# Scan levels on array quarters with idle products, squares summed on VectorE, and expert rows skipped

## The reference

```
h = rms_norm(x) * (1 + scale1) + shift1;  p = h @ w_in
# y_a: RWKV-7 time mixing, 8 heads of 64, both directions
state = state * w_t + (state @ -kk_t) (kk_t * a_t)^T + v_t k_t^T;  y_t = state @ r_t
# y_b: latent attention, 8 heads
q = rms_norm(c_q) @ w_uq;  k, v = rms_norm(c_kv) @ w_uk, w_uv;  y_b = softmax(q k^T) v @ w_o
x = x + gate1 * ((g_a * y_a + g_b * y_b) @ w_out)
# mixture of experts: 4 groups of 8, one group and then 2 experts per token
h2 = rms_norm(x) * (1 + scale2) + shift2
y_e = (silu(h2 @ w13[e][gate]) * (h2 @ w13[e][up])) @ w2[e];  x = x + gate2 * sum of 2 weighted y_e
```

## Time and profile before

| what | value |
| --- | --- |
| median of 3 runs | 2740.32 us (2726.66 to 2760.95) |
| the profiled execution | 2732.23 us, span 2730.4, mean granted TensorE clock 0.93 |
| modulation_and_norm | 0 to 137 us |
| project_in | 137 to 822 us |
| wkv_scan | 831 to 1376 us |
| mla_project | 1380 to 1566 us |
| attention | 1571 to 1886 us |
| finish_and_merge, output_and_router | 1886 to 2261 us |
| routing | 2261 to 2321 us |
| experts, 34 blocks | 2321 to 2662 us |
| end of experts, combine | 2662 to 2731 us |
| busy, whole span | PE 2433.9 us (89%), PEld 1962.5 (72%), DVE 1595.7 (58%), ACT 1062.4 (39%), POOL 677.5 (25%) |
| DMA | 433.31 MB, 122.73 MB of it written; zero stores 32 x 512 KB, 18.2 us from issue to landing |

### The profile page before, as it was taken

How to read it: one execution, slowest core, us unless ns; L and a number is a source line. 1 busy time by engine, 2 the same in 40 slices (tenths; PEclk the granted TensorE clock), 3 DMA queues, 4 the chain that set the end, 5 groups by cost and what they waited for, 6 DMA issues and landing times. The chain is left out here.

```text
span 2730.4 us, 52710 instructions
## 1 busy us (share of the span) xinstructions
PE 2433.9 (89%) x22191; PEld 1962.5 (72%) x22191; DVE 1595.7 (58%) x2165; ACT 1062.4 (39%) x1865; POOL 677.5 (25%) x498
## 2 busy tenths in 40 slices
PE   5799999999994999999979889998997994999990
PEld 2488887788884999999869756665876883666760
DVE  4444469966652354555445566666886445677756
ACT  5311133344441345445445455554122220555542
POOL 1122245545432345434213320001200000000004
PEclk8899999999995699999869989999998995999995
DMA  8422234443324132332043391103755123999977
GB/s 360 172 77 78 78 106 146 142 158 133 140 110 156 45 88 69 88 92 65 19 133 109 101 326 51 33 24 113 245 164 195 69 70 140 400 422 418 414 298 300
DMA packets 178735, 433.31 MB, mean 159 GB/s; under 512 B 38298, under 2 KB 90298, under 8 KB 160834
## 3 DMA queue, kind: packets, MB, share of 16 engines
q1 hardware_dynamic: 148548, 323.10, 34.1%
q0 software_dynamic: 15840, 57.54, 5.5%
q10 hardware_dynamic: 14112, 49.29, 4.5%
HBM read 307.15 MB, written 122.73 MB: 157 GB/s over the span
## 5 line engine op out<-in xcount | busy, mean ns | idle before, releaser
L99 PE MATMUL ps_in<-h_t_low,w_in_high 128*128 128x512 f32 x960 | 379.6, 395 | 10.5 <-POOL w_in_low L490 10.5
L100 PE MATMUL ps_in<-h_t_high,w_in_low 128*128 128x512 f32 x960 | 374.6, 390 | 0.0
L101 PE MATMUL ps_in<-h_t_high,w_in_high 128*128 128x512 f32 x960 | 374.6, 390 | 0.0
L99 PEld LDWEIGHTS ps_in<-h_t_low,w_in_high 128*128 128x128 f32 x960 | 180.7, 188 | 53.0 <-POOL w_in_low L490 11.5
L1191 POOL TENSOR_TENSOR wkv_levels<-wkv_nt,level_mask 128x1024 f32<-128x1024 f32 x60 | 140.1, 2353 | 274.5 <-ACT wkv_nt L1140 274.5
L101 PEld LDWEIGHTS ps_in<-h_t_high,w_in_high 128*128 128x128 f32 x960 | 180.6, 188 | 38.2
L100 PEld LDWEIGHTS ps_in<-h_t_high,w_in_low 128*128 128x128 f32 x960 | 180.8, 188 | 36.0
L2963 DVE TENSOR_TENSOR w_low<-w_now,w_high 128x2048 fp32r<-128x2048 f32 x64 | 146.7, 2292 | 39.3 <-ACT w_high L2800 39.3
L598 ACT COPY p_row<-ps_in 128x512 f32<-128x512 f32 x72 | 42.3, 588 | 304.5 <-PE ps_in L101 278.9
L2670 POOL DMA_INDIRECT xb<-h,row_ids x34 | 32.9, 967 | 511.1 <-PE ps_xy L2715 285.4
L488 POOL CAST w_in_high<-w_in_tile 128x1024 fp32r<-128x1024 f32 x40 | 46.6, 1164 | 335.8 <-PE ps_in L101 299.5
(11 more groups left out here) (383 smaller groups left out, 5788.9 us busy)
## 6 DMA issues: line engine op xcount, KB each, us to landing
w_now<-in_w SPq DMA_DIRECT2D x68, 1024.0 KB, 9.5
w_tile<-in_w SPq DMA_DIRECT2D x34, 1024.0 KB, 9.4
w_ada_tile<-in_w_ada SPq DMA_DIRECT2D x12, 2048.0 KB, 12.3
wkv_in<-wkv_out SPq DMA_DIRECT2D x24, 1024.0 KB, 3.9
w_in_tile<-in_w_in SPq DMA_DIRECT2D x40, 512.0 KB, 3.6
yb<-yb_tile ACTq DMA_DIRECT2D x34, 512.0 KB, 9.3
yb<-att_zeros POOLq DMA_DIRECT2D x32, 512.0 KB, 18.2
p_t<-p_mixed ACTq DMA_DIRECT2D x24, 512.0 KB, 2.7
```

The lines of the kernel that those rows point to most:

```text
L99: nc.tensor.matmul(out, w[0], x[1], start=start, stop=False)
L100: nc.tensor.matmul(out, w[1], x[0], start=False, stop=False)
L101: return nc.tensor.matmul(out, w[0], x[0], start=False, stop=stop)
```

## The change

In the scan the level products go to 32x32 quarters of the array: 64 matmuls per group instead of 32, and `lev`, `nt`, `z` and the mask become half as wide, for only the two diagonal blocks of a chunk matter at levels 0 to 4. `half_product` takes its block from `lbm`. keep_z becomes one copy, keep_nt four, first_inverse one operation. `keep_busy` issues matmuls whose results nobody reads: `idle` at j < 0 and `dense` (one) behind seven of nine groups at j >= 0. Sums of latent squares are added over the blocks on VectorE, so one matmul per sum remains. The zero stores go; `yb` is now indexed by choice and token (3072 rows), the experts' gather and a new scatter skip rows whose index is out of bounds, and combine loads plain 1 MB tiles. The merge gets 12 idle products ahead of it, routing 10 and 6. Cut to its core:

```
 def wkv_scan
-        lmask = s.sb("level_mask", [P, LEVELS, CH])
+        lmask = s.sb("level_mask", [P, LEVELS, BLK])
-        nt = s.sb("wkv_nt", [P, 2, 2 * H, CH])
-        lev = s.sb("wkv_levels", [P, LEVELS, 2 * H, CH])
+        nt = s.sb("wkv_nt", [P, 2, 2 * H, BLK])
+        lev = s.sb("wkv_levels", [P, LEVELS, 2 * H, BLK])
-        z = s.sb("wkv_z", [P, 2 * H, CH])
+        z = s.sb("wkv_z", [P, 2 * H, BLK])
...
+def keep_busy(nc, consts, out, n):
+
+    for _ in range(n):
+        nc.tensor.matmul(out, consts["ident"][:], consts["p_end"][:].rearrange("p d f n -> p (d f n)"), start=True, stop=True)
...
             def level_z(i, l):
                 for h in range(2 * H):
-                    for c in range(2):
-                        mm = nc.tensor.matmul(LV[half(c), 0, h], lev[half(c), l, h], x[half(c), i % 2, h], start=True, stop=True)
+                    for a in quads:
+                        mm = nc.tensor.matmul(LV[a, 0, h], lev[a, l, h], x[a, i % 2, h], start=True, stop=True)
                 mm.then_inc(m["z_full"], 1)
...
             def level_xz(i, l):
                 for h in range(2 * H):
-                    for c in range(2):
-                        mm = nc.tensor.matmul(LV[half(c), 1, h], z[half(c), h], xt[half(c), i % 2, h], start=True, stop=True)
+                    for a in quads:
+                        mm = nc.tensor.matmul(LV[a, 1, h], z[a, h], xt[a, i % 2, h], start=True, stop=True)
                 mm.then_inc(m["xz_full"], 1)
...
+            def idle(j, n):
+
+                if j < 0:
+                    keep_busy(nc, consts, W[:].rearrange("p h t -> p (h t)")[:, 0:2 * RF * TOK // CH], n)
+
+            def dense(j):
+
+                if j >= 0:
+                    keep_busy(nc, consts, W[:].rearrange("p h t -> p (h t)")[:, 0:2 * RF * TOK // CH], 1)
+
+            idle(-2, 20)
             for j in range(-2, N):
                 seq, inner, ahead = j >= 0, 0 <= j + 1 < N, j + 2 < N
                 if inner:
+                    idle(j, 24)
                     level_z(j + 1, 1)
+                    dense(j)
+                    idle(j, 3)
                 if seq:
                     from_state(j, 0)
                 if inner:
                     level_xz(j + 1, 1)
+                    dense(j)
+                    idle(j, 3)
                 if seq:
                     from_values(j, 0)
...
             def keep_z(i, l):
                 act.wait_ge(m["z_full"], 4 * i + l)
-                nc.scalar.mul(z[:, :, 0:BLK], LV[:, 0], blk[:, 0:1])
-                nc.scalar.mul(z[:, :, BLK:CH], LV[:, 0], blk[:, 1:2]).then_inc(m["z_kept"], 1)
+                nc.scalar.copy(z[:], LV[:, 0]).then_inc(m["z_kept"], 1)
...
             def keep_nt(i):
                 act.wait_ge(m["lbm_ready"], 4 * i + 4)
                 if i >= 2:
-                    act.wait_ge(m["half_full"], i - 1)
                     act.wait_ge(m["lev_ready"], LEVELS * (i - 1))
                 for c in range(2):
-                    ins = nc.scalar.copy(nt[half(c), i % 2].rearrange("p (d h) t -> p d h t", d=2),
-                                         lbm[half(c), i % LB].rearrange("p (d c) h t -> p d c h t", d=2)[:, :, c, :, CH * c:CH * c + CH])
+                    for b in range(2):
+                        at = CH * c + BLK * b
+                        ins = nc.scalar.copy(nt[quad(c, b), i % 2].rearrange("p (d h) t -> p d h t", d=2),
+                                             lbm[quad(c, b), i % LB].rearrange("p (d c) h t -> p d c h t", d=2)[:, :, c, :, at:at + BLK])
                 ins.then_inc(m["nt_ready"], 1)
...
-                nc.gpsimd.tensor_tensor(xt[:, i % 2], ident32[:].unsqueeze(1).to_broadcast([P, 2 * H, BLK]), lev[:, 0, :, 0:BLK], ALU.subtract).then_inc(m["x1_part"], 1)
-                pool.wait_ge(m["x1_part"], i + 1)
-                nc.gpsimd.tensor_tensor(xt[:, i % 2], xt[:, i % 2], lev[:, 0, :, BLK:CH], ALU.subtract).then_inc(m["xt_first"], 1)
+                nc.gpsimd.tensor_tensor(xt[:, i % 2], ident32[:].unsqueeze(1).to_broadcast([P, 2 * H, BLK]), lev[:, 0], ALU.subtract).then_inc(m["xt_first"], 1)
...
 def mla_project
             def latent_sums(t, b):
                 if b == 0:
-                    pe.wait_ge(m["squared"], t + 1)
+                    pe.wait_ge(m["lat_added"], t + 1)
                     if t >= 1:
                         pe.wait_ge(m["lat_var"], t)
-                first, n = ((0, QF), (QF, KVF))[b]
-                for k in range(n):
-                    at = 2 * (t % 2) + b
-                    mm = nc.tensor.matmul(ps_st[:, at:at + 1], lat_sq[:, t % 2, first + k], consts["ones"][:, 0:1], start=(k == 0), stop=(k == n - 1))
+                at = 2 * (t % 2) + b
+                mm = nc.tensor.matmul(ps_st[:, at:at + 1], lat_sum[:, t % 2, b], consts["ones"][:, 0:1], start=True, stop=True)
                 if b == 1:
                     mm.then_inc(m["sums_full"], 1)
...
+            def add_squares(t):
+                dve.wait_ge(m["squared"], t + 1)
+                if t >= 2:
+                    dve.wait_ge(m["sums_full"], t - 1)
+                for b, at in enumerate((slice(0, QF), slice(QF, L))):
+                    ins = nc.vector.tensor_reduce(lat_sum[:, t % 2, b], lat_sq[:, t % 2, at].rearrange("p k t -> p t k"), AX.X, ALU.add)
+                ins.then_inc(m["lat_added"], 1)
...
 def attention
-            nc.gpsimd.memset(zeros[:], 0.0).then_inc(zeroed, 1)
-            pool.wait_ge(zeroed, 1)
-            pool.wait_ge(v_loaded[PAIRS - 1], 16)
-            for n in range(TOK * TOP // MB, BLOCKS):
-                pool.dma_start(dram["yb"][n], zeros[:]).then_inc(zeros_stored, 16)
-            pool.wait_ge(zeros_stored, 16 * (BLOCKS - TOK * TOP // MB))
...
 def finish_and_merge
+            keep_busy(nc, consts, ps_b[:].rearrange("p f t -> p (f t)")[:, 0:2 * RF * TOK // CH], 12)
...
 def route_and_experts
+            nc.gpsimd.memset(xb[:], 0.0).then_inc(m["cleared"], 1)
+            pool.wait_ge(m["cleared"], 1)
             pool.wait_ge(m["ids"], 1)
-
-            def gather(t, b, offset):
-                pool.indirect_dma_start(out=xb[:, b], out_offset=None, in_=dram["h2"],
-                                        in_offset=bass.IndirectOffsetOnAxis(ap=offset.bitcast(U32), axis=0)).then_inc(x_in[b], 16)
-
-            for t in range(STATIC):
-                if t >= 2:
-                    pool.wait_ge(m["turned"], t - 1)
-                gather(t, t % 2, ids[:, t:t + 1])
+            rows_at = lambda offset: bass.IndirectOffsetOnAxis(ap=offset.bitcast(U32), axis=0)
+
+            def gather(b, offset):
+                pool.indirect_dma_start(out=xb[:, b], out_offset=None, in_=dram["h2"], in_offset=rows_at(offset),
+                                        bounds_check=TOK - 1, oob_is_err=False).then_inc(x_in[b], 16)
+
+            def scatter(b, offset):
+                pool.indirect_dma_start(out=dram["yb"], out_offset=rows_at(offset), in_=yb[:, b], in_offset=None,
+                                        bounds_check=TOP * TOK - 1, oob_is_err=False).then_inc(stored[b], 16)
+
+            def store(t):
+                pool.wait_ge(m["y_act"], t + 1)
+                pool.wait_ge(m["y_dve"], t + 1)
+                scatter(t % 2, row_to[:, t:t + 1])
+
+            for t in range(STATIC + 4):
+                if t < STATIC:
+                    if t >= 2:
+                        pool.wait_ge(m["turned"], t - 1)
+                    gather(t % 2, row_from[:, t:t + 1])
+                if t >= 4:
+                    store(t - 4)
...
+            def keep_busy(n):
+
+                for _ in range(n):
+                    nc.tensor.matmul(ps_xy[0][:, 0, 0:NTABLES], consts["ident"][:], consts["tables"][:], start=True, stop=True)
+
+            keep_busy(10)
             for k in range(TOP):
                 pe.wait_ge(m["hot_rows"], k + 1)
                 for c in range(T * k, T * k + T):
                     mm = nc.tensor.matmul(ps_ids[:, 0:BLOCKS], row_hot[:, c], block_hot[:, c], start=(c == 0), stop=(c == KT - 1))
             mm.then_inc(m["ids_full"], 1)
+            keep_busy(6)
...
-                act.wait_ge(m["y_act"], t + 1)
-                act.wait_ge(m["y_dve"], t + 1)
-                act.dma_start(dram["yb"][bass.ds(at, 1)].rearrange("a p d -> p (a d)"), yb[:, b]).then_inc(stored[b], 16)
...
-            do(V.scalar_tensor_tensor(out=dest, in0=blk, scalar=float(MB), in1=row, op0=ALU.mult, op1=ALU.add))
-            do(V.tensor_copy(slot[:].rearrange("p k t -> p (k t)"), dest))
             dve.wait_ge(m["ids_full"], 1)
-            V.tensor_copy(ids[:], ps_ids[:, 0:BLOCKS]).then_inc(m["ids"], 1)
+            do(V.tensor_scalar(place_part, ps_ids[:, 0:BLOCKS], 0.5, float(2 * TOP * TOK), ALU.is_lt, ALU.mult))
+            do(V.scalar_tensor_tensor(out=place, in0=ps_ids[:, 0:BLOCKS], scalar=-1.0, in1=place_part, op0=ALU.add, op1=ALU.add))
+            do(V.tensor_copy(row_to[:], place))
```

(26 more changed lines are left out.)

93 lines of the change are left out of this document (59 added, 34 removed).

## The result

The changed kernel takes 2872.7 us (median of 4 runs, 2867.0 to 2879.6), the one before 2739.3 in the same comparison: ratio 1.049, 95% interval 1.043 to 1.055. Forecast were 2655. The profiled executions have spans of 2873.0 and 2730.4, 142.6 apart.

| stage | before | after | moved | forecast |
| --- | --- | --- | --- | --- |
| wkv_scan | 548.9 | 692.9 | +144.0 | -54 |
| mla_project | 191.6 | 184.7 | -6.9 | -13.5 |
| attention | 315.0 | 315.3 | +0.3 | -1 |
| finish_and_merge | 182.7 | 184.5 | +1.8 | -1.5 |
| output_and_router | 192.0 | 192.6 | +0.6 | 0 |

What follows compares the result with a forecast made beforehand. TensorE was taken to bound scan and experts, with a half-clock scan start. Terms -22 -32 -13.5 -1 -1.5 -5.4 -1 +0.5 -1.5 sum to -77.4, from 2732.2 to 2655 us; range 2612 to 2716.

Steps and rivals of the forecast that it cites:

- -2.0 an iteration: Steady scan: quarters save 4.8 us, seven idle products cost 2.66; over 11 iterations -22 us.
- 64 in a row: Steady scan: existing 32x32 records follow at 10 ns, 64 in a row, cited against a limit by instruction issue.
- quarters no faster per group: Rival, steady scan, 14%: issue limits quarters to 15 ns a record, 2706 us; at 30 ns +340, given 3%.
- rows 6: Profile rows of the kernel before: a 1.56 us gap put down to issue inside one 64x64 group.
- slower rival: Rival, 9%: the steady scan's clock falls because small quarters occupy the array less; half of it low gives 2810 us.
- The start: Scan start: idle products raise the clock, first iteration 54.4/1.8 = 30.1 before other terms; -20, -7 and -5, sum -32 us.
- Idle products: Steady scan: seven per iteration at 0.38 us each, 2.66 an iteration, bounds of one 0.21 and 0.60.
- The named rival: Steady scan: the clock stays high without the idle products, which cost 29 us for nothing; no chance given.
- Latent sums: Latent projection: 1.37 us a tile saved, -13.5 us; two VectorE reductions, 1.4 for both, called covered, uncovered +14.
- Merge: Merge after attention: twelve idle products warm its first products, -1.5 us, bounds 0 and -3.9.
- Routing: Routing: warm id products -4, six small VectorE operations +1.0, first block's products -1.1 and transposes -1.3; -5.4 us.
- Combine: End of kernel: twelve 1 MB loads replace 24 gathers, only the lead shortens; -1.5 us, bounds 0 and -3.

Runs made afterwards that it cites:

- kernel 4: The kernel before plus only the idle products of the scan's start, level groups still on 64x64 halves: 2720.6 us, ratio 0.993.
- kernel 1: The changed kernel with the scan of before put back, no idle products there: 2728.3 us, ratio 0.997 to the kernel before.
- 8: The changed kernel with the scan of before plus the idle products of the scan's start: 2701.9 us, ratio 0.990 to the kernel before.
- experiment 12: The kernel before, on halves, plus idle products at the scan's start and behind seven groups of each steady iteration: 2749.0 us, ratio 1.004.
- 3: The kernel before with only its eight level groups moved to 32x32 quarters, no idle products: 2856.1 us, ratio 1.041.
- 13: The changed kernel with the scan of before on bfloat16 halves, plus start and steady idle products: 2624.5 us, ratio 0.960 to the kernel before.
- 14: The same kernel as 13 with its eight level groups on 32x32 quarters: 2646.0 us, ratio 0.967 to the kernel before.
- 10: The kernel before with the scan's level tiles in bfloat16, on 64x64 halves, no idle products: 2682.5 us, ratio 0.980.
- 6: The kernel before with all eight level groups on 32x32 quarters and their tiles in bfloat16: 2690.1 us, ratio 0.985.
- experiment 9: The kernel before with only two level groups (z of levels 1 and 3) on 32x32 quarters: 2809.6 us, ratio 1.027.

## Why the prediction was wrong

**The step that failed** is "-2.0 an iteration": it priced a level group on quarters by the 0.68 us of L992 and L1002 taken twice, with nothing for the supply of instructions. The runs showed +14.4 an iteration in its place. As a price of the array this was right and even high, 1.22 with what stands between groups (1.17 without) instead of 1.36. But those two groups are 128 instructions each with slower groups around them, and eight of 256 are another demand. What the array no longer needed, the supply of instructions did. The step in the text, "64 in a row" as evidence against a limit of issue, took a short burst for a rate. An iteration by parts: 38.2, less 8 x 0.72 for the groups, plus 3.7 for the idle products, is 36.1; 9.3 are gaps; the remaining 8.3 of 53.7 is put down to half clock, by difference. It fits: a mean of 0.81 is 38% of the time at 0.50, 20 us, and at the ratio of 1.8 of the earlier trace rows an estimated 9 of them would fall away at full clock. Eleven times 53.7 - 39.3 is 158, of which the start gives back 15.

The signs were in the trace before. The rival "quarters no faster per group" named issue as the cause and rows 6 as its sign, and was given 14% and a price of 15 ns a record, 1.94 us a group, at full clock; its extreme of 30 ns a record, +340, is a slip: 128 records at 30 ns are 3.84 us, 1.90 over the 1.94 of now, and 88 times that is +167. Its mechanism was right, its form wrong: it is a limit of all instructions, not of a group's records, so a group breaks off wherever the supply ends, and the clock follows. The slower rival had the clock at 9% and 2810. Each held a half of the loss; that both come from one cause, so that their prices add up, was not seen. What I could have worked out: 16 KB fetches, 8 in one iteration of before and a quickest interval of 3.2 us, against an iteration of 3,148 instructions, 12.3 fetches, 39 us, where I forecast 36. The gap of 1.56 us in the earlier trace rows was itself such a stop; it ends 2.4 us after a fetch began.

**The start** was forecast at -32: the closing group before the second iteration came at 902.7 instead of 918.1, -15, and the second iteration, forecast at 38 less 2, starved. Without quarters the same products gave 16.6 us in kernel 4, and about 20 between kernels 1 and 8 (8.9 and 29.4 under the kernel before of their own comparison). So the direction held, the size did not: the 54.4/1.8 took the whole iteration for TensorE's work, while some is waiting for masks and copies that no clock shortens.

**Idle products** were forecast at 0.38 us and cost 0.53. The named rival, that the steady ones do nothing, was right on float32. That it came out at the price that I gave (28 for 29) is partly luck: at 0.53 each the seven cost 41 us, and other iterations happened to be shorter (experiment 12).

**Latent sums**: forecast 1.37 a tile. A tile gains 0.41. I called VectorE's 1.4 us covered, because it is busy 100 of 186 us; but the two reductions, 1.88 us together, stand ahead of the heads' work in its queue and TensorE now waits 0.7 a tile for it. In the last tile with sums, when VectorE has no more squares to add, the tile takes 11.70: the relief of TensorE was sized right, and what was called covered was not. A busy share says nothing of the queue. Half of the stage's 7 to 8 us is one early tile, which took 12.4 instead of 16.3.

**Attention**: 0.3 for -1, nothing. **Merge**: +1.8 for -1.5 (in kernel 1's trace the stage takes 181.1, -1.6, so neither is sure). The idle products run, the first products are at full clock, but the second group is cold again at 2037.13, as TensorE waits 5.18 us for VectorE's branch_low ahead of it:

```profile
2031.56 0.39 PE L101 MATMUL ps_branch<-branch_high,w_o_high 128*128 128x512 f32 x1
2037.13 0.77 PE L99 MATMUL ps_branch<-branch_low,w_o_high 128*128 128x512 f32 x1 [5.18 <-DVE branch_low L2268]
```

**Routing**: forecast -4 for warm id products. Ten idle products took 8.88 us and raised the clock (0.85 on average), but ended 2.60 us before the id products' turn, and the 48 ran at 0.57 again and took 9.30 (10.49 in the earlier trace rows).

```profile
2418.03 8.88 PE L2761 MATMUL ps_xy<-tables,ident 128*128 128x439 f32 x20
2429.51 9.30 PE L2767 MATMUL ps_ids<-route_block_hot,route_row_hot 128*128 128x56 f32 x48 [2.60 <-DVEq L2997]
```

**Experts**: as forecast, 336.55 us of TensorE in 339, at DMA 0.94; the relief there showed nothing. **Combine**: forecast 1.5 sooner; its first VectorE operation comes 11.2 us after the stage's begin instead of 9.3. It waits for the gate broadcast, which GpSimd now issues while SP's loads of 1 MB are under way and which takes 10.1 us in the chain of waits; its median from issue to landing is 9.1 us, and was 4.5. That move had no price in my sum.

```profile
2824.29 1.28 DVE L3132 SCALAR_TENSOR_TENSOR mixed<-picked,weight,mixed 128x1024 f32<-128x1024 f32 x1 [24.15 <-DMA gate_broadcast<-mod_rows]
```

**Open**: that fetches are late because the scan's loads fill the DMA engines, which is half of the gaps with two quarter groups, was read from the times and not tried, for example by moving those loads. Why the clock falls as far with 21 stops as with 36 (0.78 and 0.79) was not looked into. How much of the 8.3 us of half clock would stay in float32 if no instructions were missing was not tried; bfloat16 took its place.

## What to carry to other kernels

Count TensorE's instructions beside its busy time: float32 matmuls of small tiles are four instructions each, and here nothing under about 14 ns each could be kept up, which the scan on 64x64 tiles used to about three quarters (2,096 instructions in 38.2 us) and a group on 32x32 tiles exceeds threefold. The count must fit locally, block by block, and not on average over an iteration. To split a matmul in order to fill the array makes sense only while that supply holds; the larger tile was better in two of the three pairs here (before and 3, 13 and 14) and no worse in the third (10 and 6). Idle products pay where TensorE waits for other engines at half clock, as at the scan's start or in kernel 13, and cost their full time where it is packed or short of instructions.

## What the runs showed of the hardware

Instructions arrive 16 KB, 256 of TensorE's, at a time, never closer than 3.2 us in sixteen traces, 3.5 to 3.8 where it is starved (20 fetches in a row at 3.78 in kernel 3). When a fetch begins, at most 297 are left, and what it brings was used 2.15 us later at the earliest (experiment 3). TensorE stops in mid-group for up to 4.9 us when they run out, which the profile shows as idle time ended by "issue"; the stops over 3 us are those in which the fetch itself began late, with the DMA engines busy (experiment 9). An idle product of 192 columns costs 0.53 us in a packed stream, not the 0.32 of its two records.
